# Weight halves on ScalarE after the modulation sums, and VectorE's first low part after the norm, at the start of a fused two-block transformer kernel

## The chip, the cores and the metric

The kernel runs on one core of one Trainium2 chip. The metric is the device time of one execution in microseconds (us), the median of several runs. TensorE does the matmuls (PE in the rows, its weight loads PEld), VectorE is DVE, ScalarE is ACT, GpSimd is POOL, and SyncE (SP) issues most of the DMAs.

## The reference, cut to what matters

Batch 1, 256 tokens, width 1024. Two hybrid layers are followed by a neighbourhood-attention layer with a feed-forward block and by a latent-attention layer with a mixture of 8 experts. Each layer begins like this; the change lies in the first one (l = 0):

```python
cs = silu(c)                                    # c: (1, 1024)
mod = cs @ w_ada[l] + b_ada[l]                  # (1, 3072): shift, scale, gate
h = rmsnorm(x, g_pre[l]) * (1.0 + scale) + shift
u = h @ w_in[l]                                 # the projections of the mixer
...                                             # attention, then y @ w_out[l]
x = x + gate * rmsnorm(y, g_post[l])
```

## The kernel before, in words

All weights come from HBM in steps of 1 MB (128x2048 floats) through a ring of six tiles `raw`. SyncE issues the step that reuses a tile once VectorE has counted up `raw_used` for its last user. A step is one of two kinds.

A step of kind "w" is half of a weight slot (4 of the 8 blocks of 128 rows). For precision it is split: ScalarE writes `w_hi` (`hi_to`, L1625), VectorE writes the rest `w_lo` = raw - w_hi (`raw_to`, L2217), and TensorE does three matmuls for each product (`mm3`, L833 to L835): high by high, low by high, high by low. `w_hi` and `w_lo` have three places (SPL = 3); ScalarE writes a place again when TensorE has counted `split_used`. The activations are split in the same way into `h_hi` and `h_lo`.

A step of kind "ada" is half of a 512-wide piece j of `w_ada`. VectorE multiplies it by `cs` and adds it up in four instructions (L2233, L2235), TensorE adds over the partitions (`ada`, L903), and ScalarE copies the sums into `modc` (`ada_out`, L1680). The pieces share one PSUM bank, so TensorE starts piece j only when ScalarE has copied piece j-1.

The program starts with phase "pre": eight ada steps, pieces 0 to 3, which are the shift and the scale of the first layer. Then phase "lay0" takes its own steps: w 0, w 1, w 2, half of ada 4, w 3, the other half, w 4, and so on. Between them lies the norm. VectorE scales x by 1/rms (`normed`, L2257, once GpSimd has written it at L739), TensorE turns it, `make_ab` (L2294 to L2300) forms the scale and shift columns from `modc`, and then ScalarE (`h_hi`, L1654 and L1658) and VectorE (`norm`, L2276 and L2268) make `h_hi` and `h_lo` by turns. TensorE's first projection (`feat_slot(0, ..., fresh=True)`) needs w 0 in both parts and `h_lo` in its first two quarters.

Every engine runs its instructions in the order in which this file writes them; nothing is planned at run time. ScalarE and VectorE each keep a count `done` of the steps already issued, so a later call such as `hi_to(5)` or `split_to(5)` issues only what is missing.

Of the kernel before, what the change touches and what calls it, by code (L numbers as in the profile page):

```python
# [20 lines left out]
SPL = 3  # L21
# [371 lines left out]
def build(nc, dram):  # L393
    ctx = ExitStack()
    with ctx:
# [1216 lines left out]
        def _(act):  # L1612
            a = nc.scalar
            e = Count(sg)
            done = [0]

            def hi_to(n):

                for i in range(done[0], min(n, SPLITS[e.phase])):
                    step = STEP_OF_SPLIT[e.phase][i]  # L1620
                    r = RAW_AT[e.phase][step]
                    act.wait_ge(*e.at(f"raw_in{r}", sum(q == r for q in RAW_AT[e.phase][:step + 1]), 16))
                    if SPL_NEED[e.phase][i] is not None:
                        act.wait_ge(*e.at("split_used", SPL_NEED[e.phase][i]))
                    a.activation(wh[:, SPL_AT[e.phase][i], :], raw[:, r, :], ACT.Copy).then_inc(*e.inc("hi"))  # L1625
                done[0] = max(done[0], min(n, SPLITS[e.phase]))
# [49 lines left out]
            def ada_out(j, buf):  # L1676
                act.wait_ge(*e.at("ada_sum", PARTS[e.phase].index(j) + 1))
                j6 = j % 6
                if j6 < 4:
                    ins = a.activation(modc[:, buf, j6 * 4:j6 * 4 + 4], PS[:, 3, 0:4], ACT.Copy)  # L1680
                else:
                    ins = a.activation(gate[buf][:, (j6 - 4) * 512:(j6 - 3) * 512], PS[:, 3, :], ACT.Copy)
                ins.then_inc(*e.inc("bank3"))
# [123 lines left out]
            act.wait_ge(*e.at("y", 0))  # L1807
            act.dma_start(gpost[:], dram["gpost"][0]).then_inc(*e.inc("gpost", 16))
            e.resume("pre")
            ada_out(1, 1)  # L1810
            e.resume("lay0")
            hi_to(1)
            e.resume("pre")
            ada_out(2, 1)
            e.resume("lay0")
            hi_to(2)
            e.resume("pre")
            ada_out(3, 1)
            e.resume("lay0")

            def layer(l):
                unit = 6 if l == 0 else 0
# [374 lines left out]
        def _(dve):  # L2197
            v = nc.vector
            e = Count(sg)
            done = [0]  # L2200

            def link(ins):

                name = "dve" if e.phase != "end" else "dve_end"
                ins.then_inc(*e.inc(name))
                dve.wait_ge(*e.last(name))

            def raw_to(n):

                ph = e.phase  # L2210
                for i in range(done[0], min(n, len(STEPS[ph]))):
                    step, r = STEPS[ph][i], RAW_AT[ph][i]
                    if step[0] == "w":

                        s = SPL_AT[ph][step[1]]
                        dve.wait_ge(*e.at("hi", step[1] + 1))
                        v.tensor_tensor(wl[:, s, :], raw[:, r, :], wh[:, s, :].bitcast(F32),  # L2217
                                        ALU.subtract).then_inc(*e.inc("raw_used"))
                        dve.wait_ge(*e.last("raw_used"))
                    elif step[0] == "ada":  # L2220
                        _, j, kh = step
                        dve.wait_ge(*e.at(f"raw_in{r}", sum(q == r for q in RAW_AT[ph][:i + 1]), 16))
                        dst = acc[:, j % 2, :]
                        if kh == 0:
                            q = PARTS[ph].index(j)
                            if q >= 2:
                                dve.wait_ge(*e.at("ada_sum", q - 1))
                        c = cs[:, 0 if ph in ("pre", "lay0") else 1, :]
                        for k in range(4):
                            kt = kh * 4 + k  # L2230
                            w = raw[:, r, k * 512:(k + 1) * 512]
                            if kt == 0:
                                ins = v.tensor_scalar(dst, w, c[:, kt:kt + 1], None, ALU.mult)  # L2233
                            else:
                                ins = v.scalar_tensor_tensor(out=dst, in0=w, scalar=c[:, kt:kt + 1], in1=dst,  # L2235
                                                             op0=ALU.mult, op1=ALU.add)
                            if k < 3:
                                link(ins)
                            else:
                                ins.then_inc(*e.inc("raw_used"))  # L2240
                                dve.wait_ge(*e.last("raw_used"))
                    done[0] = i + 1

            def split_to(n):
                ph = e.phase
                n = min(n, SPLITS[ph])
                raw_to(STEP_OF_SPLIT[ph][n - 1] + 1)

            def start(phase, rep=0):
                e.enter(phase, rep)  # L2250
                done[0] = 0
# [244 lines left out]
            dve.wait_ge(*e.at("consts", 2))  # L2496
            link(v.scalar_tensor_tensor(out=cs[:], in0=cs[:], scalar=1.0, in1=c2, op0=ALU.add, op1=ALU.mult))
            link(v.tensor_scalar(cs[:], cs[:], 0.5, None, ALU.mult))
            raw_to(5)
            e.enter("lay0")  # L2500
            normed(xn_l)
            e.resume("pre")
# [2 lines left out]
            def layer(l):  # L2505
# [2 lines left out]
                    done[0] = 0  # L2508
                else:
                    start("lay1")  # L2510
                split_to(1)
                LP = LPS[l]
                make_ab(1, LP["bcol"], LP["gpre"])
                norm(xn_l, ab[:, 0, :], ab[:, 1, :])
# [221 lines left out]
            for l in range(2):  # L2736
                layer(l)
# [485 lines left out]
```

## Time and profile before

| | |
|---|---|
| median of 3 runs | 1628.67 us (1628.29 to 1633.32) |
| the profiled execution | 1633.32 us, span from first to last instruction 1631.4 us |
| PE busy | 1414.9 us, 87% of the span |
| DVE busy | 1216.6 us, 75% |
| ACT busy | 861.2 us, 53% |
| POOL busy | 65.3 us, 4% |
| DMA | 403.08 MB, mean 247 GB/s |

The profiled execution is the slowest of the three runs, 4.65 us above the median. All clock times below are us from the start of its span. The shares are means over stages that differ: in the first 40 us TensorE has little to do, and the DMA engines are fully busy.

### The profile page before, as it was taken

The page shows a single profiled execution, that of the slowest core. Times are in us where ns is not written, and L with a number is a line of the kernel's source. Part 1 is how long each engine was busy: PE and PEld are TensorE (multiplying, and loading weights), DVE is VectorE, ACT ScalarE, POOL GpSimd, SP SyncE. Part 2 cuts the span into 40 slices and gives each one's busy share as a digit, 9 for nine tenths or more (in the row PEclk, how much of TensorE's full clock was granted, in tenths as well). Part 3 has the DMA queues.
Part 4 walks back from the last instruction along what each step waited for, and adds up shares of the span by engine and source line. Part 5 has one row for each costly group of instructions (what it writes and reads, how often), then busy time and mean ns, then how long its engine had stood idle before and what let it go on. Part 6 is the DMA issues. An engine that isn't in the chain of part 4 may idle for free.

```text
span 1631.4 us, 21240 instructions
## 1 busy us (share of the span) xinstructions
PE 1414.9 (87%) x7628; PEld 1188.4 (73%) x7628; DVE 1216.6 (75%) x1484; ACT 861.2 (53%) x1210; POOL 65.3 (4%) x82
## 2 busy tenths in 40 slices
PE   2999878899979896899985896999999999999992
PEld 2878668787668775898964785877777777777772
DVE  7978646776485647788767535889889889899895
ACT  2434444345344534334414645677777777777772
POOL 1000000000010000000001004000000000000001
PEclk9989998899889998999987996999999999999996
DMA  9945415555165724677753214889999999999782
GB/s 398 369 173 212 173 60 197 197 209 203 52 237 217 269 78 154 253 276 290 297 201 125 102 61 153 315 335 364 355 349 355 338 353 364 342 366 362 281 361 90
DMA packets 61537, 403.08 MB, mean 247 GB/s; under 512 B 6534, under 2 KB 9734, under 8 KB 15116
## 3 DMA queue, kind: packets, MB, share of 16 engines
q1 hardware_dynamic: 52416, 379.45, 61.4%
q10 hardware_dynamic: 7020, 15.17, 2.6%
q0 software_dynamic: 2016, 7.34, 1.2%
q8 instruction: 52, 0.85, 0.2%
q14 instruction: 33, 0.27, 0.0%
HBM read 393.01 MB, written 8.91 MB: 246 GB/s over the span
## 4 chain that ended last, share of the span: by engine, by line
PE 49%; DVE 33%; ACT 10%; issue 4%; DMA 3%; POOL 1%; ACTq 0%; DVEq 0%; SPq 0%; POOLq 0%
DVE w_lo L2217 18%; PE PS L833 13%; PE PS L835 12%; PE PS L834 12%; DVE acc L2235 4%; ACT w_hi L1625 4%; DMA raw<-in_ws 2%; ACT xg L1720 2%; PE PS L986 1%; PE PS L903 1%; PE PS L1006 1%; DVE a_lo L2384 1%; PE PS L995 1%; DVE hb L2393 1%; DVE hb L2395 1%
## 5 line engine op out<-in xcount | busy, mean ns | idle before, releaser
L2217 DVE TENSOR_TENSOR w_lo<-raw,w_hi 128x2048 fp32r<-128x2048 f32 x287 | 659.6, 2298 | 150.7 <-ACT w_hi L1625 127.9
L1625 ACT ACTIVATE w_hi<-raw 128x2048 fp32r<-128x2048 f32 x287 | 548.0, 1919 | 246.0 <-PE PS L835 221.9
L833 PE MATMUL PS<-w_hi,h_hi 128*128 128x512 f32 (+2 forms) x812 | 337.3, 415 | 26.2 <-DVE h_lo L2660 8.3
L835 PE MATMUL PS<-w_hi,h_lo 128*128 128x512 f32 (+2 forms) x812 | 320.1, 394 | 0.0
L834 PE MATMUL PS<-w_lo,h_hi 128*128 128x512 f32 (+2 forms) x812 | 319.5, 393 | 0.0
L833 PE MATMUL PS<-h_hi,w_hi 128*128 128x256 f32 x776 | 234.5, 302 | 33.4 <-DVE h_lo L2268 14.4
L834 PE MATMUL PS<-h_lo,w_hi 128*128 128x256 f32 x776 | 226.8, 292 | 0.0
L835 PE MATMUL PS<-h_hi,w_lo 128*128 128x256 f32 x776 | 226.6, 292 | 0.0
L833 PEld LDWEIGHTS PS<-w_hi,h_hi 128*128 128x128 f32 x812 | 156.8, 193 | 74.4 <-DVE w_lo L2217 16.0
L2235 DVE SCALAR_TENSOR_TENSOR acc<-raw,cs,acc 128x512 f32<-128x512 f32 x252 | 189.5, 752 | 9.0
L833 PEld LDWEIGHTS PS<-h_hi,w_hi 128*128 128x128 f32 x776 | 156.2, 201 | 38.5 <-issue 11.6
L835 PEld LDWEIGHTS PS<-w_hi,h_lo 128*128 128x128 f32 x812 | 156.2, 192 | 33.1
L834 PEld LDWEIGHTS PS<-w_lo,h_hi 128*128 128x128 f32 x812 | 157.1, 193 | 29.0 <-issue 2.2
L834 PEld LDWEIGHTS PS<-h_lo,w_hi 128*128 128x128 f32 x776 | 156.2, 201 | 2.4 <-issue 1.7
L835 PEld LDWEIGHTS PS<-h_hi,w_lo 128*128 128x128 f32 x776 | 155.9, 201 | 0.0
L833 PE MATMUL PS<-w_hi,a_hi 128*128 128x512 f32 x340 | 140.0, 412 | 17.3 <-DVE a_lo L2384 11.1
L835 PE MATMUL PS<-w_hi,a_lo 128*128 128x512 f32 x340 | 134.4, 395 | 0.0
L834 PE MATMUL PS<-w_lo,a_hi 128*128 128x512 f32 x340 | 133.7, 393 | 0.0
L1886 ACT ACTIVATE lgp<-lgp,st 128x128 f32<-128x128 f32 (+1 forms) x96 | 42.9, 449 | 123.9 <-DVE st L2536 123.9
L833 PEld LDWEIGHTS PS<-w_hi,a_hi 128*128 128x128 f32 x340 | 64.4, 190 | 37.6 <-DVE w_lo L2217 23.1
L835 PEld LDWEIGHTS PS<-w_hi,a_lo 128*128 128x128 f32 x340 | 64.4, 189 | 14.6
L834 PEld LDWEIGHTS PS<-w_lo,a_hi 128*128 128x128 f32 x340 | 64.6, 190 | 11.9
(310 smaller groups left out, 1397.9 us busy)
## 6 DMA issues: line engine op xcount, KB each, us to landing
raw<-in_ws SPq DMA_DIRECT2D x359, 1024.0 KB, 5.5
y_rows<-ysb ACTq DMA_DIRECT2D x10, 512.0 KB, 7.2
rp<-in_rp ACTq DMA_DIRECT2D x8, 384.0 KB, 4.8
ckb<-in_ck ACTq DMA_DIRECT2D x2, 1024.0 KB, 6.5
y_rows<-ones ACTq DMA_DIRECT2D x3, 512.0 KB, 8.2
x<-in_x SPq DMA_DIRECT2D x1, 1024.0 KB, 13.4
gpost<-in_gpost ACTq DMA_DIRECT2D x2, 512.0 KB, 5.7
x_rows<-xn_f ACTq DMA_DIRECT2D x2, 512.0 KB, 3.8
```

The costliest lines, as they stand in the source:

```text
L833: t.matmul(out, lhs[0], rhs[0], start=start, stop=False, skip_group_check=True)
L834: t.matmul(out, lhs[0], rhs[1], start=False, stop=False, skip_group_check=True)
L835: return t.matmul(out, lhs[1], rhs[0], start=False, stop=stop, skip_group_check=True)
L903: last = t.matmul(PS[:, 3, c:c + 1], a[:, c * P:(c + 1) * P], ones[:, 0:1], start=True, stop=True)
L986: t.matmul(PS[:, PS_S[i % 2], 0:2 * u["nk"]].rearrange("p (a k) -> p a k", a=2), u["q"], u["k"], start=True, stop=True).then_inc(*e.inc("s ...
L995: last = t.transpose(PS[:, PS_PT, c * P:(c + 1) * P], lgp[:, i % 3, c * P:(c + 1) * P], ident)
L1006: last = t.matmul(PS[:, PS_O, h * HD:(h + 1) * HD], ptp[:, i % 2, (a * n + c) * P:(a * n + c + 1) * P], u["v"][a][c], start=c == 0, stop=c ...
L1625: a.activation(wh[:, SPL_AT[e.phase][i], :], raw[:, r, :], ACT.Copy).then_inc(*e.inc("hi"))
L1720: ins = a.activation(xg[:, kt, :], PS[:, 6 + kt // 4, (kt % 4) * P:(kt % 4 + 1) * P], ACT.Identity, scale=ab[:, 0, kt:kt + 1], bias=ab[:, ...
L1886: a.activation(part, part, ACT.Exp, bias=mn(c), scale=-1.0, accum_out=sm(c)).then_inc(*e.inc("probs"))
L2217: v.tensor_tensor(wl[:, s, :], raw[:, r, :], wh[:, s, :].bitcast(F32), ALU.subtract).then_inc(*e.inc("raw_used"))
L2235: ins = v.scalar_tensor_tensor(out=dst, in0=w, scalar=c[:, kt:kt + 1], in1=dst, op0=ALU.mult, op1=ALU.add)
```

## The change

In the first layer ScalarE copies the sums of pieces 1, 2 and 3 first and then writes `w_hi` of w 0, w 1 and w 2 in a row, all ahead of its part of the norm. VectorE scales x after four ada steps instead of five, and writes `w_lo` of w 0 after the norm, with w 1 and w 2, instead of ahead of `make_ab`. The second layer is as it was.

```diff
@@ ScalarE
             e.resume("pre")
-            ada_out(1, 1)
+            for j in range(1, 4):
+                ada_out(j, 1)
             e.resume("lay0")
-            hi_to(1)
-            e.resume("pre")
-            ada_out(2, 1)
-            e.resume("lay0")
-            hi_to(2)
-            e.resume("pre")
-            ada_out(3, 1)
-            e.resume("lay0")
+            hi_to(SPL)
@@ VectorE
-            raw_to(5)
+            raw_to(4)
             e.enter("lay0")
             normed(xn_l)
...
                 else:
                     start("lay1")
-                split_to(1)
+                    split_to(1)
                 LP = LPS[l]
                 make_ab(1, LP["bcol"], LP["gpre"])
```

On ScalarE, from the squares of x to the norm, the order changes as follows (modc is the copy of a piece's sums, w_hi the high part of a weight half, hb and h_hi the norm).

```order
 L1639 ACTIVATE xn_l,st<-x 128x1024 x2
 L1808 DMA gpost<-in_gpost 128x1024
-L1680 ACTIVATE modc<-PS 128x4
-L1625 ACTIVATE w_hi<-raw 128x2048
-L1680 ACTIVATE modc<-PS 128x4
-L1625 ACTIVATE w_hi<-raw 128x2048
-L1680 ACTIVATE modc<-PS 128x4
+L1680 ACTIVATE modc<-PS 128x4 x3
+L1625 ACTIVATE w_hi<-raw 128x2048 x3
 L1654 ACTIVATE hb<-PS,ab 128x256 x2
 L1658 ACTIVATE h_hi<-hb 128x512 x2
```

Two w_hi stood between the copies and none between the last copy and the norm; now three stand there. The third is the one that stood behind the norm.

On VectorE, from the fifth ada step to the first low part behind the norm, before:

```order
7 L2233 TENSOR_SCALAR acc<-raw,cs 128x512
8 L2235 SCALAR_TENSOR_TENSOR acc<-raw,cs,acc 128x512 x3
9 L2257 TENSOR_SCALAR xn_l<-x,st 128x1024 x2
10 L2235 SCALAR_TENSOR_TENSOR acc<-raw,cs,acc 128x512 x4
11 L2233 TENSOR_SCALAR acc<-raw,cs 128x512
12 L2235 SCALAR_TENSOR_TENSOR acc<-raw,cs,acc 128x512 x7
13 L2217 TENSOR_TENSOR w_lo<-raw,w_hi 128x2048
14 L2294 TENSOR_TENSOR modc<-modc,par 128x16
18 L2268 TENSOR_TENSOR h_lo<-hb,h_hi 128x512
20 L2268 TENSOR_TENSOR h_lo<-hb,h_hi 128x512 x3
21 L2217 TENSOR_TENSOR w_lo<-raw,w_hi 128x2048 x2
```

The same place after the change (its line numbers are six lower):

```order
7 L2251 TENSOR_SCALAR xn_l<-x,st 128x1024 x2
8 L2227 TENSOR_SCALAR acc<-raw,cs 128x512
9 L2229 SCALAR_TENSOR_TENSOR acc<-raw,cs,acc 128x512 x7
10 L2227 TENSOR_SCALAR acc<-raw,cs 128x512
11 L2229 SCALAR_TENSOR_TENSOR acc<-raw,cs,acc 128x512 x7
12 L2288 TENSOR_TENSOR modc<-modc,par 128x16
16 L2262 TENSOR_TENSOR h_lo<-hb,h_hi 128x512
18 L2262 TENSOR_TENSOR h_lo<-hb,h_hi 128x512 x3
19 L2211 TENSOR_TENSOR w_lo<-raw,w_hi 128x2048 x3
```

The scaling of x moved ahead of the fifth ada step, and the one w_lo of row 13 moved behind the last h_lo.

## Rows read from the trace of the kernel before

**Rows 1.** Chain of waits, 0 to 130 us: start, us, what.
```profile
33.89 1.52 ACT w_hi L1625
35.41 0.30 issue
...
44.62 2.30 DVE w_lo L2217
```

**Rows 2.** ScalarE in order of time: start, duration, what, idle before and releaser.
```profile
31.40 1.91 ACT L1625 ACTIVATE w_hi<-raw 128x2048 fp32r<-128x2048 f32 x1 [10.66 <-DMA raw<-in_ws]
33.89 1.91 ACT L1625 ACTIVATE w_hi<-raw 128x2048 fp32r<-128x2048 f32 x1 [0.52 <-DMA raw<-in_ws]
35.71 0.15 ACT L1680 ACTIVATE modc<-PS 128x4 f32<-128x4 f32 x1
36.58 1.02 ACT L1654 ACTIVATE hb<-PS,ab 128x256 f32<-128x256 f32 x2 [0.72 <-DVE ab L2300]
37.74 1.15 ACT L1658 ACTIVATE h_hi<-hb 128x512 fp32r<-128x512 f32 x2
...
49.44 1.92 ACT L1625 ACTIVATE w_hi<-raw 128x2048 fp32r<-128x2048 f32 x1 [4.07 <-PE PS L835]
55.20 1.92 ACT L1625 ACTIVATE w_hi<-raw 128x2048 fp32r<-128x2048 f32 x1 [3.84 <-PE PS L835]
```

**Rows 3.** VectorE in order of time, 17 to 60 us.
```profile
19.09 0.49 DVE L2233 TENSOR_SCALAR acc<-raw,cs 128x512 f32<-128x512 f32 x1 [0.48 <-DMA raw<-in_ws]
21.98 1.54 DVE L2257 TENSOR_SCALAR xn_l<-x,st 128x1024 f32<-128x1024 f32 x2
27.23 5.48 DVE L2235 SCALAR_TENSOR_TENSOR acc<-raw,cs,acc 128x512 f32<-128x512 f32 x7
33.41 2.29 DVE L2217 TENSOR_TENSOR w_lo<-raw,w_hi 128x2048 fp32r<-128x2048 f32 x1 [0.71 <-ACT w_hi L1625]
35.97 0.17 DVE L2294 TENSOR_TENSOR modc<-modc,par 128x16 f32<-128x16 f32 x1 [0.26 <-ACT modc L1680]
36.58 1.12 DVE L2276 TENSOR_SCALAR hb<-PS,ab 128x256 f32<-128x256 f32 x2
38.47 0.69 DVE L2268 TENSOR_TENSOR h_lo<-hb,h_hi 128x512 fp32r<-128x512 f32 x1 [0.77 <-ACT h_hi L1658]
43.16 1.42 DVE L2268 TENSOR_TENSOR h_lo<-hb,h_hi 128x512 fp32r<-128x512 f32 x2 [2.12 <-ACT h_hi L1658]
44.62 4.62 DVE L2217 TENSOR_TENSOR w_lo<-raw,w_hi 128x2048 fp32r<-128x2048 f32 x2
49.27 0.49 DVE L2233 TENSOR_SCALAR acc<-raw,cs 128x512 f32<-128x512 f32 x1
52.16 2.29 DVE L2217 TENSOR_TENSOR w_lo<-raw,w_hi 128x2048 fp32r<-128x2048 f32 x1
57.63 2.29 DVE L2217 TENSOR_TENSOR w_lo<-raw,w_hi 128x2048 fp32r<-128x2048 f32 x1
```

**Rows 4.** TensorE and GpSimd in order of time.
```profile
18.66 1.87 PE L903 MATMUL PS<-ones,acc 128*128 128x1 f32 x8 [4.11 <-DVE acc L2235]
19.37 0.77 POOL L739 TENSOR_TENSOR st<-st 128x2 f32<-128x2 f32 x1 [0.18 <-POOL st L734]
41.20 0.55 PE L833 MATMUL PS<-h_hi,w_hi 128*128 128x256 f32 x1 [5.84 <-DVE h_lo L2268]
43.25 0.41 PE L833 MATMUL PS<-h_hi,w_hi 128*128 128x256 f32 x1
47.02 0.28 PE L833 MATMUL PS<-h_hi,w_hi 128*128 128x256 f32 x1
```

**Rows 5.** Issues of raw, 0 to 60 us.
```profile
DMA to landing us min/median/max: 5.3/11.5/17.8
```

**Rows 6.** Mean granted TensorE clock of the execution.
```profile
core 0: 1631.4 us, clock 0.940
```

**Rows 7.** Stretches: us, busy us of each engine, PEclk, DMA share, GB/s.
```profile
40.00:50.00 10.00, 8.80 (x55) 8.84 (x56) 7.68 (x8) 4.42 (x6) 0.00 (x0) 1.00 1.00 392
100.00:110.00 10.00, 8.11 (x39) 6.29 (x38) 6.74 (x14) 2.45 (x7) 0.00 (x0) 0.83 0.66 250
110.00:120.00 10.00, 9.36 (x48) 8.83 (x49) 6.65 (x14) 3.96 (x8) 0.00 (x0) 0.66 0.30 107
```

## The prediction

> **What bounds the kernel now.** I read the chain of waits for the first 130 us, because the change lies there and nowhere else. In it [rows 1] the reader is to see two things. Ahead of the norm the chain runs over ScalarE's w_hi of w 1 and the copy that stands behind it. Behind the norm it runs over VectorE's w_lo. Then I read the two engines in order of time. ScalarE waits for the transfers of w 0 and w 1 (10.66 and 0.52 us idle), so both w_hi lie in time that it has free, and its last copy of sums starts at 35.71 [rows 2]. VectorE ends the ada steps at 27.23 + 5.48 = 32.71, and writes w_lo of w 0 from 33.41 to 35.70 while that last copy is still to come: `make_ab` starts at 35.97 and was released by the copy [rows 3]. So the w_lo of w 0 costs nothing today. From 43.16 VectorE shows no idle time up to 57.63 and beyond: each row starts where the one before it ends [rows 3]. TensorE starts its first projection at 41.20, released by the second h_lo [rows 4], and w 0 occupies it until ScalarE's w_hi of w 3 is released at 49.44, 8.24 us; w 1 takes until 55.20, 5.76 us [rows 2]. In this stage VectorE and TensorE are both nearly full, so a late start there has no slack to vanish in.
>
> **The change part by part.**
>
> *Scaling of x ahead of the fifth ada step.* VectorE is free at about 18.6. It started the fifth step at 19.09, after 0.48 us for a transfer [rows 3]. Now it waits for GpSimd, which ends at 19.37 + 0.77 = 20.14 [rows 4], with 0.1 us for the release (w_hi's end 33.31 to w_lo's start 33.41 [rows 2, 3]): 20.25. The work from there to the end of the ada steps is the same as before, 32.71 - 19.09 = 13.62 us, so it ends at 33.87, 1.16 us later. TensorE turns x earlier, which nobody waits for.
>
> *Copies ahead of the w_hi.* The last sum took TensorE 1.87 us from 0.06 us after VectorE's step [rows 4]: now from 33.93 to 35.80. The copy starts at about 35.85, where it stood at 35.71 [rows 2]. Before, this sum waited for a copy behind w_hi of w 0; that wait goes, and what is late in its place is VectorE. `make_ab` starts at about 36.1 against 35.97 [rows 3]: nothing won, 0.1 us lost.
>
> *Three w_hi between the last copy and the norm.* This is the first large term. From 36.0 ScalarE issues three; one starts 1.82 us after the other (33.89 to 35.71 is such a distance [rows 2]), 5.46 us in all, to 41.46. Its part of the norm then starts at 41.46 and not at 36.58: 4.88 us late. VectorE's hb is long done, so the small wait of h_hi for it (37.60 to 37.74 [rows 2]) goes: 4.7 us remain. `ab` and the first hb give no cover; VectorE stands still for those 4.7 us in front of its first h_lo, which was at 38.47 [rows 3]. The norm alternates between the two engines, so all of it shifts by 4.7: the last h_lo ends at 43.16 + 1.42 + 4.7 = 49.3.
>
> *w_lo of w 0 behind the norm.* This is the second. TensorE could start at 41.20 + 4.7 = 45.9 by the activations. It now needs w_lo of w 0, which VectorE writes only from 49.3, behind two h_lo that TensorE did not need for its start: until 51.6. TensorE starts at 51.65, 10.45 us late.
>
> *What VectorE does with it.* It owes three w_lo (3 x 2.33) and half an ada (52.16 - 49.27 = 2.89 [rows 3]), 9.9 us, and is at w 3 at 59.2, which is 7.0 us late. But w_hi of w 3 needs TensorE to be through with w 0: 51.65 + 8.24 = 59.9, and 2.0 us for w_hi: 61.9, against 52.16. So VectorE is held for 2.7 us and is 9.75 late. For w 4 the two come out together: TensorE ends w 1 at 65.65, w_hi at 67.65; VectorE's own path gives 61.9 + 5.47 = 67.4. So w_lo of w 4 starts at 67.65 against 57.63: 10.0 us late. From there VectorE's stream is 10.0 late and TensorE's 10.45, and they wait for each other at the attention; I take 10.1.
>
> *Transfers.* SyncE stands in order. The step behind w 0's tile (w 4) goes out at 51.6, not 35.7, and all later ones queue behind it. At the best landing time of the stretch, 5.3 us [rows 5], it is there at 56.9, and ScalarE wants it at 65.65: no cost. At the longest, 17.8 us [rows 5], it lands at 69.4: 3.8 us more. The long times belong to a fully busy stretch (DMA share 1.00 at 40 to 50 [rows 7]); now the queue has run dry by then, so I take the short end.
>
> *The half clock at the restart.* The first matmuls last 0.41 us, later ones 0.28 [rows 4]: TensorE starts w 0 at the lower of its two levels, 1.2 GHz, after a gap of 5.8 us, though the stretch's mean shows 1.00. The slow part is in the 8.24. After a gap of 16 us it may come out longer or shorter. If w 0 took only 5.76, w_hi of w 3 would come 2.5 us sooner and the loss would end at 7.5 (VectorE's own 7.0, then the wait at w 4). If it were slow throughout, 8.24 becomes some 10.3, and the loss 12.2. I take the measured 8.24.
> The Trainium skill ("TensorE: Matmul & The Clock Gate", Part 1: The HAM clock gate) says that sustained activity restores the rate and that the number of slow matmuls differs between runs of one kernel. The slow first matmuls here agree; that the number differs no run here shows yet. It puts no further charge on a longer gap, so by it the sum stays.
>
> **Sum.** 4.7 (norm late by ScalarE) + 5.75 (TensorE's extra wait for w_lo, 51.65 - 45.9) = 10.45 on TensorE, of which 0.35 is given back in waits for VectorE: +10.1 us. On the profiled execution that is 1633.32 + 10.1 = 1643.4. It lies 4.65 above the median of the three runs, so for the median: 1628.67 + 10.1 = 1638.8, 0.6% slower. Later stages run the same instructions on a ring that holds six steps; nothing in them ends at a fixed time, so nothing gives the lag back.
>
> **Rivals.**
>
> *VectorE alone sets the loss.* If w_hi of w 3 is never waited for, VectorE's own delay is all: 4.7 + 2.33 = 7.0, 1635.7. For it: VectorE had no idle time from 43 on. Against it: even the present slack at w 3 is under 1 us (w_hi ends at 51.36, w_lo starts at 52.16 [rows 2, 3]), and TensorE is now 3.4 us further back than VectorE.
>
> *A late transfer adds to it.* w 4, issued 16 us later, lands late: up to +3.8, 1642.6. For it: one order for all steps on SyncE. Against it: nearly 9 us of margin at the short landing.
>
> *Not slower: the clock gives it back.* The granted clock is 0.83 and 0.66 at 100 to 120 us [rows 7], 5.1 us worth of full rate, and its mean over the span is 0.940 [rows 6], which is 98 us worth. If these stretches fall elsewhere once all is shifted and cost 10 us less on the path, the time is 1628 to 1629. It decides where the mean clock comes out at about 0.946. If only the 5.1 us of the first layer vanish, +5.0, 1633.7, at the edge. For it: the three runs of one kernel spread by 5.0 us. Against it: there is no reason for a shift to lower the sum, it may as well raise it.
>
> *The change does nothing on the path.* The order shows three w_hi ahead of the norm and w_lo of w 0 behind it on in-order engines; no row lets this be free. I give it no chance of its own.
>
> **How the numbers follow.** The forecast with its clock bounds, +7.5 to +12.2 (1636.2 to 1640.9): 0.80. VectorE alone, 1635.7: 0.07. A late transfer, up to 1642.6: 0.07. The clock gives back: 0.06, of which 0.02 faster by over 0.3% and 0.04 within. 0.3% (4.9 us, about what a measurement here can tell from no change) is below all the other cases, so slower has 0.94. The range takes in the second and third case and the spread between runs: 1634.5 to 1643.5.
>
> **What would show it.** In the new profile: the last copy of sums near 35.85 and three w_hi in a row from 36.0; ScalarE's hb at 41.5; VectorE idle some 4.7 us more ahead of its first h_lo; w_lo of w 0 near 49.3 and TensorE's first projection matmul near 51.65, released by that w_lo; the w_lo of w 3 idle before it by 2 to 3 us and released by w_hi; w_lo of w 4 near 67.65; the DMA share at 40 to 50 well under 1. The rest of the trace should be the same, 10 us later. I am wrong on the mechanism if TensorE starts before 49, or if a transfer releases w_hi of w 3 or w 4. I am wrong on the size if the lag at 90 us is 10 but the end shows another: then the later stages, or the clock, gave or took.

## The result, and the profile after

The changed kernel is slower. The first reading was 1642.36 us (median of 4 runs, 1639.86 to 1644.54) against 1628.48 us (4 runs of before); the ratio is 1.0074, 95% interval 1.0054 to 1.0092. A second reading on another occasion gave 1640.2 us (6 runs) against 1629.95 us (29 runs), ratio 1.0077, interval 1.0059 to 1.0095. The ratios here are those on record; they are estimated from the runs and are not exactly the quotients of the two medians (1.0085 and 1.0063 for these two). Taken together, the 29 runs on record of the changed kernel have a mean of 1641.3 us (1636.33 to 1644.97), and the 73 runs of before that were timed beside the experiments below one of 1630.4: 10.9 us apart, with a standard error of 0.6. Forecast were 1638.8 us and +10.1. The profiled execution took 1639.46 us, span 1637.6.

The place of the change first: ScalarE in order of time, changed kernel (columns as in [rows 2]).

```profile
28.85 0.17 ACT L1680 ACTIVATE modc<-PS 128x4 f32<-128x4 f32 x1 [8.04 <-PE PS L903]
35.69 0.17 ACT L1680 ACTIVATE modc<-PS 128x4 f32<-128x4 f32 x1 [6.67 <-PE PS L903]
35.76 5.50 ACT L1625 ACTIVATE w_hi<-raw 128x2048 fp32r<-128x2048 f32 x3
41.16 1.01 ACT L1654 ACTIVATE hb<-PS,ab 128x256 f32<-128x256 f32 x2
...
59.88 1.92 ACT L1625 ACTIVATE w_hi<-raw 128x2048 fp32r<-128x2048 f32 x1 [11.99 <-PE PS L835]
65.64 1.92 ACT L1625 ACTIVATE w_hi<-raw 128x2048 fp32r<-128x2048 f32 x1 [3.84 <-PE PS L835]
```

The last copy of sums stands where it stood (35.69, before 35.71), so taking the copies first won nothing. Behind it the three w_hi fill 5.50 us, and the norm's first hb starts at 41.16, 4.58 us after its old place [rows 2]. VectorE in order of time:

```profile
20.13 1.54 DVE L2251 TENSOR_SCALAR xn_l<-x,st 128x1024 f32<-128x1024 f32 x2 [1.45 <-POOL st L739]
28.26 5.48 DVE L2229 SCALAR_TENSOR_TENSOR acc<-raw,cs,acc 128x512 f32<-128x512 f32 x7
35.97 0.18 DVE L2288 TENSOR_TENSOR modc<-modc,par 128x16 f32<-128x16 f32 x1 [2.23 <-ACT modc L1680]
42.79 0.69 DVE L2262 TENSOR_TENSOR h_lo<-hb,h_hi 128x512 fp32r<-128x512 f32 x1 [5.08 <-ACT h_hi L1658]
47.90 1.42 DVE L2262 TENSOR_TENSOR h_lo<-hb,h_hi 128x512 fp32r<-128x512 f32 x2 [2.54 <-ACT h_hi L1658]
49.36 6.95 DVE L2211 TENSOR_TENSOR w_lo<-raw,w_hi 128x2048 fp32r<-128x2048 f32 x3
61.90 2.29 DVE L2211 TENSOR_TENSOR w_lo<-raw,w_hi 128x2048 fp32r<-128x2048 f32 x1 [2.72 <-ACT w_hi L1625]
67.66 2.29 DVE L2211 TENSOR_TENSOR w_lo<-raw,w_hi 128x2048 fp32r<-128x2048 f32 x1 [0.32 <-ACT w_hi L1625]
```

Against [rows 3]: `make_ab` is on time and now waits 2.23 us, in the place that held w_lo of w 0. The first h_lo waits 5.08 us for ScalarE instead of 0.77. The three w_lo follow the norm; the w_lo of w 3 waits 2.72 us for w_hi and starts at 61.90 (before 52.16), that of w 4 at 67.66 (57.63): 10.03 us late. TensorE:

```profile
51.70 0.58 PE L833 MATMUL PS<-h_hi,w_hi 128*128 128x256 f32 x1 [16.05 <-DVE w_lo L2211]
52.51 0.41 PE L833 MATMUL PS<-h_hi,w_hi 128*128 128x256 f32 x1
56.76 0.28 PE L833 MATMUL PS<-h_hi,w_hi 128*128 128x256 f32 x1
```

It stood idle for 16.05 us instead of 5.84 [rows 4], and its releaser is no longer an h_lo but w_lo. w 0 took from 51.70 to 59.88, 8.18 us, nearly the 8.24 of before. The transfers, in stretches of 10 us:

```profile
40.00:50.00 10.00, 0.00 (x0) 0.00 (x0) 4.50 (x7) 5.26 (x9) 0.00 (x0) 0.50 0.60 225
50.00:60.00 10.00, 8.30 (x52) 8.30 (x53) 8.98 (x7) 0.12 (x1) 0.00 (x0) 0.68 0.74 274
```

The DMA share at 40 to 50 is 0.60 where it was 1.00 [rows 7]: the queue ran dry, as the next step (w 4) takes w 0's tile, whose w_lo is now written only from 49.36 on, and all later steps are issued behind it. No w_hi of w 3 or w 4 was released by a transfer.

So the 10.03 us of lag at 68 us are accounted for. At the end the two profiled spans lie only 6.2 us apart (1637.6 and 1631.4). The `make_ab` rows of the later stages show where the lag moves. Before:

```profile
244.51 0.17 DVE L2294 TENSOR_TENSOR modc<-modc,par 128x16 f32<-128x16 f32 x1
455.73 0.18 DVE L2294 TENSOR_TENSOR modc<-modc,par 128x16 f32<-128x16 f32 x1
622.83 0.17 DVE L2294 TENSOR_TENSOR modc<-modc,par 128x16 f32<-128x16 f32 x1
863.06 0.17 DVE L2294 TENSOR_TENSOR modc<-modc,par 128x16 f32<-128x16 f32 x1
```

After:

```profile
251.98 0.18 DVE L2288 TENSOR_TENSOR modc<-modc,par 128x16 f32<-128x16 f32 x1
460.09 0.17 DVE L2288 TENSOR_TENSOR modc<-modc,par 128x16 f32<-128x16 f32 x1
629.11 0.18 DVE L2288 TENSOR_TENSOR modc<-modc,par 128x16 f32<-128x16 f32 x1
869.78 0.18 DVE L2288 TENSOR_TENSOR modc<-modc,par 128x16 f32<-128x16 f32 x1
```

The lag is 7.5, 4.4, 6.3, 6.7 us. The granted clock of the stretch goes the same way; 95 to 250 us, before and then after:

```profile
95.00:250.00 155.00, 133.75 (x740) 110.44 (x739) 101.95 (x191) 70.34 (x152) 3.17 (x6) 0.91 0.42 153
```

```profile
95.00:250.00 155.00, 139.40 (x779) 112.85 (x777) 102.84 (x210) 69.56 (x168) 1.49 (x4) 0.96 0.41 152
```

0.91 against 0.96: the profiled execution of before had more of the low level there, and it was the longest of its runs (1633.32 us). Over the whole span it is the other way round, 0.940 in before and 0.935 in the changed kernel. Whether the new order or chance does this is what the delays below (the third and the tenth kernel) are for.

### The profile page after: what moved, and what is told of

It is laid out like the page before. It is cut to its first block, busy times and chain, and to the rows that moved or that the text cites. A ratio compares the mean times of both kernels' runs of the same rounds, so it can differ in the third digit from the quotient of the medians.

```text
span 1637.6 us, 21240 instructions
## 1 busy us (share of the span) xinstructions
PE 1412.2 (86%) x7628; PEld 1185.4 (72%) x7628; DVE 1215.8 (74%) x1484; ACT 860.8 (53%) x1210; POOL 65.3 (4%) x82
## 4 chain that ended last, share of the span: by engine, by line
PE 49%; DVE 32%; ACT 10%; issue 5%; DMA 2%; POOL 1%; ACTq 0%; DVEq 0%; SPq 0%; POOLq 0%
DVE w_lo L2211 18%; PE PS L833 13%; PE PS L835 12%; PE PS L834 12%; ACT w_hi L1625 4%; DVE acc L2229 4%; ACT xg L1720 2%; PE PS L903 1%; PE PS L986 1%; PE PS L1006 1%; DVE a_lo L2378 1%; DVE hb L2387 1%; DVE hb L2389 1%; DVE h_lo L2344 1%; PE PS L995 1%
```

## The experiments

All were timed beside runs of the kernel before on the same chip. "Lag" is the start of VectorE's w_lo of w 4 less 57.63, the start in the first profile of before.

**1. w_lo of w 0 back ahead of make_ab** (the changed kernel, one line)

```diff
                 else:
                     start("lay1")
-                    split_to(1)
+                split_to(1)
```

> The changed kernel with one line put back: VectorE writes w_lo of w 0 ahead of make_ab again, ScalarE keeps its three w_hi ahead of the norm. Theory (two terms in series: ScalarE's w_hi in front of the norm, then VectorE's w_lo behind it): TensorE's first projection starts near 45.5 instead of 51.7, w_lo of w 3 near 56.9 without a wait for w_hi, w_lo of w 4 near 62.4, 4.7 us behind the kernel before; run time 4.7 us above before, give or take 3 for what the clock does later. Rival (the place of w_lo is all of it): w_lo of w 4 is back at 57.6 and the run at the time of before. Rival (the w_hi are all of it): w_lo of w 4 stays at 67.7.

Measured: 1636.04 us (12 runs) against 1630.72 (23 runs), ratio 1.0026, interval 1.0011 to 1.0041. VectorE:

```profile
37.72 2.29 DVE L2211 TENSOR_TENSOR w_lo<-raw,w_hi 128x2048 fp32r<-128x2048 f32 x1 [4.03 <-ACT w_hi L1625]
...
48.88 4.62 DVE L2211 TENSOR_TENSOR w_lo<-raw,w_hi 128x2048 fp32r<-128x2048 f32 x2
56.42 2.29 DVE L2211 TENSOR_TENSOR w_lo<-raw,w_hi 128x2048 fp32r<-128x2048 f32 x1
61.90 2.29 DVE L2211 TENSOR_TENSOR w_lo<-raw,w_hi 128x2048 fp32r<-128x2048 f32 x1
```

TensorE:

```profile
45.47 0.55 PE L833 MATMUL PS<-h_hi,w_hi 128*128 128x256 f32 x1 [9.86 <-DVE h_lo L2262]
48.59 0.32 PE L835 MATMUL PS<-h_hi,w_lo 128*128 128x256 f32 x1
```

w_lo of w 0 fits wholly into time in which VectorE waits for ScalarE. TensorE starts at 45.47, released by an h_lo again; w 3 has no wait, the lag is 4.27 us. Both rivals (0 and 10) fall. The forecast was 4.7; the last h_lo ended 0.47 us earlier than in the changed kernel (48.85 against 49.32). Why the third h_lo starts about 0.4 us later in the kernels that have w_lo of w 0 behind the norm is left open.

**2. ScalarE's old order back, VectorE as changed**

```diff
             e.resume("pre")
-            for j in range(1, 4):
-                ada_out(j, 1)
+            ada_out(1, 1)
             e.resume("lay0")
-            hi_to(SPL)
+            hi_to(1)
+            e.resume("pre")
+            ada_out(2, 1)
+            e.resume("lay0")
+            hi_to(2)
+            e.resume("pre")
+            ada_out(3, 1)
+            e.resume("lay0")
```

> The changed kernel with ScalarE's order of before put back (w_hi of w 0 and w 1 between the copies, the third behind the norm); VectorE as changed, w_lo of w 0 behind the norm. Theory: the norm is on time (last h_lo ends at 44.6), w_lo of w 0 runs 44.6 to 46.9, TensorE's first projection starts at 47.0, w_lo of w 3 waits for w_hi until 57.2, w_lo of w 4 starts near 63.0, 5.4 us behind before; run time 5.4 us above before, give or take 3. Rival (VectorE's own 2.3 us are all this part costs): w_lo of w 3 starts at 54.5 and w 4 at 60.0 without a wait. Rival (the w_hi are all of it): nothing is late.

Measured: 1637.15 us (11 runs) against 1630.72 (23), ratio 1.0042, interval 1.0027 to 1.0058.

```profile
45.13 6.95 DVE L2217 TENSOR_TENSOR w_lo<-raw,w_hi 128x2048 fp32r<-128x2048 f32 x3
56.95 2.29 DVE L2217 TENSOR_TENSOR w_lo<-raw,w_hi 128x2048 fp32r<-128x2048 f32 x1 [1.99 <-ACT w_hi L1625]
62.72 2.29 DVE L2217 TENSOR_TENSOR w_lo<-raw,w_hi 128x2048 fp32r<-128x2048 f32 x1 [0.32 <-ACT w_hi L1625]
```

The wait of w 3 for w_hi is there, the lag is 5.09. The one more w_lo that VectorE now owes behind the norm costs 2.3 us by itself; the rest comes by TensorE, which starts at 47.48, and the w_hi behind it:

```profile
47.48 0.58 PE L833 MATMUL PS<-h_hi,w_hi 128*128 128x256 f32 x1 [11.73 <-DVE w_lo L2217]
54.94 1.91 ACT L1625 ACTIVATE w_hi<-raw 128x2048 fp32r<-128x2048 f32 x1 [9.47 <-PE PS L835]
```

The two parts are 4.27 and 5.09, together 9.36; both at once give 10.03. The missing 0.67 is in w 0's time on TensorE: 7.46 us here (13 matmuls of 0.4 us or more), 8.18 in the changed kernel (21 of them).

**3. A pure delay of 9.3 us in the kernel before**

```diff
+                if l == 0:
+                    dve.wait_ge(*e.at("hi", 1))
+                    for _ in range(4):
+                        link(v.tensor_tensor(wl[:, 0, :], raw[:, 2, :], wh[:, 0, :].bitcast(F32), ALU.subtract))
                 split_to(1)
```

> The kernel before with a pure delay: VectorE writes w_lo of w 0 four times more ahead of make_ab, 4 x 2.32 = 9.3 us, everything else in its old order. Theory (a lag at the start costs just itself, and what the run adds or takes beyond it is where the clock's low stretches fall): make_ab at 45.3, w_lo of w 4 at 66.9, 9.3 us behind; the medians of this kernel and of the changed one lie within 4 us of each other, and a single run may lie 3 to 5 us off its landmark's lag. Rival (the changed kernel's 13.9 us contain some 4 us that its new order causes later on): this one stays at 9.3 above before, 1637.8, with a spread as small as before.

Measured: 1639.56 us (6 runs, 1638.33 to 1640.67) against 1630.72 (23), ratio 1.0056, interval 1.0036 to 1.0076.

```profile
33.63 9.27 DVE L2514 TENSOR_TENSOR w_lo<-raw,w_hi 128x2048 fp32r<-128x2048 f32 x4 [0.70 <-ACT w_hi L1625]
67.36 2.29 DVE L2217 TENSOR_TENSOR w_lo<-raw,w_hi 128x2048 fp32r<-128x2048 f32 x1
```

The w_lo of w 4 starts at 67.36, a lag of 9.73, and the median lies 8.84 us above before (the mean 9.2). That is what theory and rival both said of this kernel, so it does not tell them apart; it shows that a plain delay is carried to the end. What speaks on the rival is the changed kernel again, below.

**10. The same with two instead of four**, 4.6 us

> The kernel before with a pure delay of two extra w_lo of w 0 ahead of make_ab, 2 x 2.32 = 4.6 us. Theory (a lag at the start is carried to the end one for one, on the mean over runs): w_lo of w 4 near 62.4, 4.7 behind before, and the mean time 3.5 to 6.5 us above before. Rival (a lag is partly swallowed, or some microseconds are added, by what the clock does later): the mean lies outside that.

Measured: 1637.05 us (10 runs) against 1631.26 (21), ratio 1.0038, interval 1.0025 to 1.0050.

```profile
62.89 2.29 DVE L2217 TENSOR_TENSOR w_lo<-raw,w_hi 128x2048 fp32r<-128x2048 f32 x1
```

Lag 5.26: this execution began 0.8 us late (its first w_lo at 34.25, not 33.41), and the mean lies 5.8 us above before. A plain delay costs what it is long, here as at 9.3 us. The changed kernel has a lag of 10.03 and a mean 10.9 above before, give or take 0.6: a second cause in the new order of 4 us, as the third kernel's rival had it, is ruled out; one of about 1 us is not.

**5. The changed kernel once more**

> The changed kernel as it is, once more, beside more runs of the kernel before. Theory (the start costs 10 us and the rest of the first reading's 13.9 is how low-clock stretches fell in a few runs): w_lo of w 4 at 67.7 again to 0.2 us, while the end of the run differs by some us from the first profile; the difference of the medians comes out nearer 10 than 14. Rival (the new order costs some 4 us more behind the start): it stays at 13 to 14 against many runs of before.

Measured: 1640.2 us (6 runs, 1636.47 to 1643.81) against 1629.95 (29 runs, 1624.96 to 1635.14). w_lo of w 4 at 67.74. The medians differ by 10.25 us, the means by 10.8. The later `make_ab` rows stand within 0.2 us of the first profile's (252.13, 460.26, 629.25, 869.88), and the two spans lie 0.3 us apart, where I had expected some microseconds: the course of an execution can repeat. The single runs of one kernel still spread over 7 to 10 us. My median of before rested on three runs, two of which lay near 1628.5.

**4. Matmuls to warm up TensorE, in the changed kernel**

```diff
+                if l == 0:
+                    pe.wait_ge(*e.at("h", 2))
+                    for _ in range(36):
+                        t.matmul(PS[:, 0, 0:S], hh[:, 0, 0:P], hh[:, 1, :], start=True, stop=True,
+                                 skip_group_check=True)
                 feat_slot(0, LAY_BANK[0:2], fresh=True)
```

> The changed kernel with 36 extra matmuls of 256 columns on TensorE, from the second h_lo on (about 45.4), in time in which it stands idle; their output is overwritten. Theory: some 22 of them take the slow pitch of 0.21 us and the rest 0.12, they end near 51.8, w 0 then runs at full rate in 5.8 us and not 8.2, w_hi of w 3 is done at 59.6, w_lo of w 3 starts at 59.5 instead of 61.9 and w 4 near 65.4 instead of 67.7: 2.3 us of the lag are gone, because of TensorE's restart at 1.2 GHz. Rival (VectorE's own order sets the lag and the restart does not matter): w_lo of w 4 stays at 67.7. Rival (the slow start goes with the first matmuls on fresh data and not with the gap): w 0 keeps its 8.2 us.

Measured: 1639.94 us (7 runs) against 1630.72 (23), ratio 1.0051, interval 1.0031 to 1.0071.

```profile
59.89 2.29 DVE L2216 TENSOR_TENSOR w_lo<-raw,w_hi 128x2048 fp32r<-128x2048 f32 x1 [0.66 <-ACT w_hi L1630]
65.65 2.29 DVE L2216 TENSOR_TENSOR w_lo<-raw,w_hi 128x2048 fp32r<-128x2048 f32 x1 [0.32 <-ACT w_hi L1630]
```

```profile
45.48 6.54 PE L1057 MATMUL PS<-h_hi 128*128 128x256 f32 x36 [9.76 <-DVE h_lo L2267]
51.85 0.29 PE L833 MATMUL PS<-h_hi,w_hi 128*128 128x256 f32 x1
```

The extra matmuls ran from 45.48, w 0 took 6.0 us (51.85 to w_hi of w 3 at 57.87), and 2.0 of the 10.0 us of lag are gone. The first matmuls on w 0 now last 0.29 us and less, so the slow restart belongs to the gap and not to the fresh data. In the timed runs 2 us are hard to tell: the mean of 7 lies 9.0 us above before.

**6 to 8. The kernel before with VectorE's gap filled, with the warm-up, and with both.** The gap:

```diff
                 lo(1)
+                if e.phase == "lay0":
+                    split_to(2)
                 lo(2)
```

The warm-up is that of the fourth kernel with 30 matmuls that read w_hi of w 0, behind `pe.wait_ge(*e.at("hi", 1))`.

> The kernel before with one move: VectorE writes w_lo of w 1 between the second and the third h_lo of the first layer, where it stands idle for 2.12 us. Theory (TensorE's w 0, with its slow start, is the next bound right behind VectorE): w_lo of w 3 starts at 51.4 instead of 52.16, held by w_hi, w 4 near 57.2 instead of 57.63: only 0.4 to 0.8 us of the 2.1 us are won; run time as before. Rival (VectorE alone sets the pace): w 4 at 55.5.

> The kernel before with 30 extra matmuls of 256 columns between the last sum and the first projection, output overwritten. Theory: w 0 runs at full rate in 5.8 us and not 8.2, w_hi of w 3 starts at 47.0 instead of 49.4, but VectorE is busy until 52.16, so w_lo of w 3 and w 4 stay at 52.2 and 57.6: nothing won at VectorE; run time as before. Rival (TensorE's start sets the pace): w 4 near 55.

> Both edits on the kernel before: the w_lo of w 1 in VectorE's gap and the 30 extra matmuls. Theory (two bounds side by side; only together do they give way): w_lo of w 3 at 50.1, w 4 at 55.5, 2.1 us ahead of before, more than the sum of the two alone; run time 2 us below before, under what a few runs can tell. Rival: the gains add up as in the single edits, w 4 at 57.2.

Measured, against 1629.95 us (29 runs), 12 runs each: gap 1629.68, ratio 1.0009 (0.9996 to 1.0022); warm-up 1632.8, ratio 1.0022 (1.0008 to 1.0036); both 1630.28, ratio 1.0008 (0.9994 to 1.0022). The w_lo of w 4 starts at 57.22 in the first, at 57.82 in the second and at 56.04 in the third. The first row is of the gap alone, the second of the warm-up alone:

```profile
57.22 2.29 DVE L2217 TENSOR_TENSOR w_lo<-raw,w_hi 128x2048 fp32r<-128x2048 f32 x1 [0.32 <-ACT w_hi L1625]
57.82 2.29 DVE L2222 TENSOR_TENSOR w_lo<-raw,w_hi 128x2048 fp32r<-128x2048 f32 x1
```

The gap alone moves it by 0.41 of 2.1 us, held by w_hi; the warm-up alone does not move it, as VectorE itself is busy until then; both together win 1.59 us, more than the sum, but 0.5 less than expected. The row of the kernel with both that tells why:

```profile
45.36 2.29 DVE L2222 TENSOR_TENSOR w_lo<-raw,w_hi 128x2048 fp32r<-128x2048 f32 x1 [0.65 <-ACT w_hi L1630]
```

I had forgotten w_hi of w 2: ScalarE writes it only behind its norm, to 45.3. The kernel with the warm-up alone is slower than before by 2.7 us on the mean, though its w_lo of w 4 is on time to 0.2 us; its expectation, a time as before, missed. That is not explained.

**9. Both edits of the eighth kernel and a third: w_hi of w 2 in ScalarE's own gap** (shown is the third)

```diff
                 hi(1)
+                if e.phase == "lay0":
+                    hi_to(3)
                 scaled(3)
```

> The kernel before with both edits of the last run and a third: ScalarE writes w_hi of w 2 in its own gap of 2.63 us between the second and third quarter of the norm (the changed kernel had it ahead of the norm, where it cost 1.8 us). Theory (a step costs nothing only where its engine waits anyway): the norm stays on time, w_lo of w 2 starts at 45.0 without the 0.65 us wait of the last run, w 3 near 50.2, w 4 near 55.6, 2 us ahead of before; run time 1629 to 1630 mean against 1630 to 1631, not to be told from before with a spread of 2.5 us per run. Rival (w_hi of w 2 again delays the norm): the third h_lo starts after 43.6, and w 4 at 56.0 or later.

Measured: 1628.12 us (12 runs, 1627.31 to 1633.45) against 1631.26 (21), ratio 0.9985, interval 0.9974 to 0.9997.

```profile
38.63 1.90 ACT L1630 ACTIVATE w_hi<-raw 128x2048 fp32r<-128x2048 f32 x1
```

```profile
43.24 1.42 DVE L2275 TENSOR_TENSOR h_lo<-hb,h_hi 128x512 fp32r<-128x512 f32 x2
44.69 2.29 DVE L2224 TENSOR_TENSOR w_lo<-raw,w_hi 128x2048 fp32r<-128x2048 f32 x1
49.90 2.29 DVE L2224 TENSOR_TENSOR w_lo<-raw,w_hi 128x2048 fp32r<-128x2048 f32 x1
55.38 2.29 DVE L2224 TENSOR_TENSOR w_lo<-raw,w_hi 128x2048 fp32r<-128x2048 f32 x1
```

The norm is on time, no w_lo waits, and w 4 starts 2.25 us ahead of before. It is the one version whose interval lies below 1, by 0.15% in the ratio, under the 0.3% that I held to be measurable. Among ten versions one such interval is weak evidence; the gain of 2.25 us is shown by the trace, at w 4, and not by the times.

The lag beside the difference of the mean times, each against the runs of before that were timed beside it:

| kernel | lag at w 4, us | mean, us above before |
|---|---|---|
| three gaps | -2.25 | -2.0 |
| gap and warm-up | -1.59 | +0.7 |
| gap | -0.41 | +0.6 |
| warm-up | +0.19 | +2.7 |
| w_lo back | +4.27 | +4.5 |
| w_hi back | +5.09 | +6.7 |
| small delay | +5.26 | +5.8 |
| changed, warm | +8.02 | +9.0 |
| delay | +9.73 | +9.2 |
| changed, second reading | +10.11 | +10.8 |

Eight agree to 1.6 us; two lie 2.3 and 2.5 above. A single run spreads by mostly 2 to 3 us (standard deviation), so a mean of 12 is good to about 1 against before: the two are more than I would put down to chance with confidence. Both have the warm-up, but so have three gaps and changed, warm, which agree to 0.2 and 1.0; the warm-up is not shown to be the cause. Nine of the ten lie above their lag, by 1.0 us on the mean of all ten. The lags are counted from a single execution of before, so an offset of that execution would show like this; no run here settles it.

## Why the prediction was right

*What bounds the kernel.* Right: both engines carried the late start through the stage without giving any back up to 94 us (the first logits at 94.53, where they were at 84.50 in the execution of [rows 3]).

*Scaling of x earlier.* Right in sign and of no account: the ada steps ended at 33.74, 1.0 later, and I had said 1.16.

*Copies first.* Right that nothing is won: make_ab at 35.97, I had said 36.1.

*Three w_hi ahead of the norm.* Right: hb at 41.16, said 41.46. Shown by the second kernel, which takes them away: its hb starts at 36.67.

*w_lo behind the norm.* Right: TensorE at 51.70, said 51.65. Shown by the first kernel. That the cost is by way of TensorE and the wait at w 3 (2.72 us, said 2.7), and not VectorE's own 2.3 us, is shown by the wait for w_hi in the second kernel (1.99 us), and by its absence in the first.

*Transfers.* Right that none was late.

*The restart.* The 8.24 us stayed at 8.18 after the longer gap: 22 matmuls of 0.4 us or more in before (41.20 to 46.02), 21 in the changed kernel (51.70 to 56.35). That they were nearly the same is luck, for in the first experiment it was 14 (45.47 to 48.59) and in the second 13, after gaps of 9.9 and 11.7 us. The same slow restart stood in before, and there it cost nothing: the warm-up of the seventh kernel did not move w 4. In the changed kernel TensorE is on the path, and it costs 2.0 of the 10 us, as the fourth kernel shows. The Trainium skill ("TensorE: Matmul & The Clock Gate", Part 1: The HAM clock gate) says that the number of slow matmuls differs between runs of one kernel. Two executions of the changed kernel do not show it, with 21 each; but the 30 extra matmuls of the seventh and the eighth kernel, in which nothing differs until VectorE's added w_lo at 40.96, took 5.22 us in one and 6.50 in the other, and that agrees.

*The sum.* Its terms were right: hb 4.58 us late (4.88 forecast), TensorE 10.50 (10.45), w 4 on VectorE 10.03 (10.0). At the end the first reading gave 13.9 and the second 10.25; all runs together give 10.9. The term that was off is the base: I took the kernel before at 1628.67 from three runs, and with 20 to 30 runs it is 1630 to 1631.3, with single runs from 1625 to 1635. So the time of the first reading, 1642.36, lies above the forecast with its clock bounds (1636.2 to 1640.9, chance 0.80), in what I had kept for a late transfer, and no transfer was late. That the range still held it is owed to its width and not to the working.

The rival that the clock gives the lag back describes a real thing, the low stretches of 95 to 250 us; there the lag of the profiled pair falls by 2.6 us, while the granted clock reads 0.91 and 0.96. But the mean clock of the profiled execution came out at 0.935, not at 0.946, and the two delays show that on the mean nothing like 10 us is given back. Nor does the mean clock tell the time: of the 23 runs recorded with the first reading the fastest (1636.33) has 0.936 and the slowest (1644.97) 0.939. The other rivals fell: VectorE alone would show no wait at w 3, and a late transfer would show as a releaser.

## What to carry to other kernels

A step costs nothing only in the gap it was in: before moving one, look at what its engine waits for there and at the next thing queued behind its new place. Here two w_hi and a w_lo stood in waits, and a third w_hi stood behind the norm, where nothing waited for it; all four were moved onto the only path. When two engines alternate, filling a gap of one of them pays only up to the bound of the other; gains that are next to nothing apart (0.4 and none) can be real together (1.6 us).

For a change worth a few microseconds, compare the same instruction in two traces, which repeats to about 0.2 us once an execution's own first microseconds are taken out; the total needs some twenty runs of each: with a spread of 2.5 us per run that is good to about 0.8 us.

## What the runs showed of the hardware that was not expected

The granted clock in the profile's stretches can miss the low level (1.2 GHz of 2.4). In before it reads 1.00 for 40 to 50 us [rows 7], while the matmuls there last 0.41 us until 46.0 [rows 4]. In the changed kernel the same slow pitch stands in a stretch that reads 0.50 (53 to 55 us, 11 matmuls in 2 us, against 19 at 57 to 59):

```profile
53.00:55.00 2.00, 2.00 (x11) 2.00 (x11) 1.97 (x2) 0.00 (x0) 0.00 (x0) 0.50 0.67 274
57.00:59.00 2.00, 2.00 (x19) 2.00 (x18) 1.93 (x3) 0.00 (x0) 0.00 (x0) 1.00 0.97 393
```

At a restart here the durations or the count of the matmuls tell the level where the granted clock does not.

One kernel on one core, with nothing else changed, spread from 1624.96 to 1635.14 us over 29 runs: 0.6%, as much as the whole effect of this change.
